# The gates' chain as steps inside the projection, and the adaLN products moved from VectorE to ScalarE and GpSimd

## What is computed

```
mod = silu(c) @ w_ada + b_ada                      # six sections of 1024 columns
z = h @ w_in + b_in                                # h: the normed tokens, 1024 + 256 context
q, k, v, o, gt, ga, gb = split(z)
gates = gt + b_gate                                # log i and forget pre-activations, two directions
u = ga * sigmoid(gb)                               # input of a 31 tap depthwise convolution
y = conv(u) + conv_b
lf = log_sigmoid(forget);  b = cumsum(lf) in each chunk of 128;  E = log i - b
# running maxima of E, a recurrence over the 10 chunks for the stabiliser m, and then
# exp(...) of four combinations: these are what the chunks of the mLSTM need
```

## Time and profile before

| | |
|---|---|
| median of 3 runs | 3208.84 us (3199.12 to 3208.93) |
| the profiled execution's time | 3209.92 us |
| its span | 3207.3 us |
| PE busy | 2741.5 us, 85% |
| DVE, ACT, POOL busy | 1672.9, 1164.2, 841.9 us |

### The profile page before, as it was taken

The page is one execution under the profiler, slowest core; times in us unless marked ns, Lnnn a source line. Parts: engine busy times, 40 slices in busy tenths (PEclk is TensorE's granted clock), DMA queues, the critical chain, the costliest instruction groups (busy, mean ns, idle before and its releaser), DMA issues. The chain is left out here.

```text
span 3207.3 us, 38552 instructions
## 1 busy us (share of the span) xinstructions
PE 2741.5 (85%) x11990; PEld 1944.7 (61%) x11991; DVE 1672.9 (52%) x2474; ACT 1164.2 (36%) x1598; POOL 841.9 (26%) x1036
## 2 busy tenths in 40 slices
PE   4899969497869999999999965999968999874997
PEld 4455435375357777777777753446654666763776
DVE  3667856565356567576576533145462111445653
ACT  1100023332056566566665542026322111214653
POOL 0100023221734334334333321067120000104333
PEclk9999966697989999999999987999989999976999
DMA  6331100133268788888798745000201110416972
GB/s 224 106 105 56 56 0 1 52 126 145 76 221 276 230 275 273 272 301 284 245 328 275 237 112 202 26 1 2 42 14 50 49 40 20 152 76 240 312 227 51
DMA packets 159179, 463.43 MB, mean 144 GB/s; under 512 B 37964, under 2 KB 67264, under 8 KB 138328
## 3 DMA queue, kind: packets, MB, share of 16 engines
q1 hardware_dynamic: 115816, 358.12, 30.1%
q0 software_dynamic: 43264, 104.02, 13.6%
HBM read 414.31 MB, written 91.62 MB: 158 GB/s over the span
## 5 line engine op out<-in xcount | busy, mean ns | idle before, releaser
L1855 DVE TENSOR_TENSOR moe_low<-moe_raw,moe_high 128x2048 fp32r<-128x2048 f32 x160 | 359.6, 2289 | 81.2 <-ACT moe_high L1800 81.2
L1765 PE MATMUL psum<-moe_high,moe_xg_high 128*128 128x512 f32 x960 | 390.2, 406 | 7.3 <-DVE moe_xg_low L1860 3.0
L1767 PE MATMUL psum<-moe_high,moe_xg_low 128*128 128x512 f32 x960 | 378.3, 394 | 0.0
L1766 PE MATMUL psum<-moe_low,moe_xg_high 128*128 128x512 f32 x960 | 375.7, 391 | 0.0
L1800 ACT ACTIVATE moe_high<-moe_raw 128x2048 fp32r<-128x2048 f32 x160 | 297.6, 1915 | 0.1
L1701 POOL DMA_INDIRECT moe_acc<-moe_y_blk,moe_is_now x97 | 214.5, 2211 | 299.4 <-DMA moe_acc<-moe_y_blk,moe_is_now 267.6
L1812 ACT ACTIVATE moe_y_blk<-psum,row_w 128x1024 f32 x124 | 138.2, 1115 | 235.6 <-DMA moe_acc<-moe_y_blk,moe_is_now 125.9
L1739 PE MATMUL psum<-ident,moe_xg 128*128 128x128 f32 x976 | 135.8, 284 | 95.2 <-DMA moe_xg<-moe_rows,moe_ig_now 95.0
L1752 PE MATMUL psum<-moe_high_down,moe_hid_high 128*128 x488 | 207.3, 425 | 11.6 <-DVE moe_hid_low L1864 10.7
L1765 PEld LDWEIGHTS psum<-moe_high,moe_xg_high 128*128 128x128 f32 x960 | 181.6, 189 | 44.8 <-issue 5.9
L1767 PEld LDWEIGHTS psum<-moe_high,moe_xg_low 128*128 128x128 f32 x960 | 181.0, 189 | 43.2
(11 more groups left out here) (578 smaller groups left out, 5043.2 us busy)
## 6 DMA issues: line engine op xcount, KB each, us to landing
moe_raw<-in_we_gate SPq DMA_DIRECT2D x64, 1024.0 KB, 7.8
moe_raw<-in_we_up SPq DMA_DIRECT2D x64, 1024.0 KB, 11.0
moe_raw<-in_we_down SPq DMA_DIRECT2D x64, 1024.0 KB, 7.6
moe_raw<-in_w_e_gate SPq DMA_DIRECT2D x16, 1024.0 KB, 6.9
moe_raw<-in_w_e_up SPq DMA_DIRECT2D x16, 1024.0 KB, 9.9
moe_raw<-in_w_e_down SPq DMA_DIRECT2D x16, 1024.0 KB, 8.2
w_ring<-in_w_in SPq DMA_DIRECT2D x12, 1024.0 KB, 7.6
wada<-in_w_ada SPq DMA_DIRECT2D x8, 1024.0 KB, 10.7
```

What stands on the lines that cost most here:

```text
L1765: pe.matmul(to, x_hi, R(of_k(w_hi, k)), start=(k == 0), stop=False)
L1766: pe.matmul(to, x_hi, R(of_k(w_lo, k)), start=False, stop=False)
L1767: last = pe.matmul(to, x_lo, R(of_k(w_hi, k)), start=False, stop=(k == KD - 1))
L1855: dve.tensor_tensor(R(low[:, at:at + 2048]), raw[r][:, part], hi, ALU.subtract).then_inc(w_low, 1)
```

## The change

`multiply` moves to ScalarE: it scales each of a half's four pieces into one of two `products` buffers, and signals. A new `add` on GpSimd copies or adds each product into `part`. GpSimd does the `add` of half q-2 in `load`, ahead of the DMA of half q. The two slots and the products now lie in `s.x` (tiles 2 to 6) and not in a buffer of their own; as `sig_o` uses tiles 4 to 7 of `s.x`, DVE waits for the last add before the first o entry. The gain row gets two buffers.

The plan changes: ADA4 stands behind v0 and gt0, ADA5 and ADA6 in channel group 2, ADA7 behind v5 and gt5, and group 3 has no ada entry. Between group 3's four tiles and behind them stand four new entries, `gate` 0 to 3. They hold what `stage_gates` did, cut at PE's steps (class `Gates`; the arithmetic is the same, its buffers lie in `hcT`): the gather and the logarithms run behind the last gt. `stage_gates` and its block are gone.

```diff
--- before.py
+++ after.py
@@ class LaterSections @@
-    def __init__(self, s, at, slots, part, gain_row):
-        self.s, self.at, self.slots, self.part, self.gain_row = s, at, slots, part, gain_row
+    def __init__(self, s, at, slots, products, part, gain_row):
+        self.s, self.at, self.slots, self.products, self.part, self.gain_row = s, at, slots, products, part, gain_row
+        self.product_ready, self.added = sem(s, "ada_product_ready"), sem(s, "ada_added")
         self.ada_in = [sem(s, f"ada_in{i}") for i in range(2)]
-        self.rows_in, self.gain_in = sem(s, "ada_rows_in"), sem(s, "ada_gain_in")
+        self.rows_in, self.gain_in = sem(s, "ada_rows_in"), [sem(s, f"ada_gain_in{i}") for i in range(2)]
         self.ada_used, self.finished = sem(s, "ada_used"), sem(s, "ada_finished")
 
...
         for q in range(2 * self.TILES):
             j, kh = divmod(q, 2)
             if q >= 2:
-
+                self.add(pool, q - 2)
                 pool.wait_ge(self.ada_used, q - 1)
             c0 = 2 * D + j * 512
             pool.dma_start(self.slots[q % 2], src[kh][:, :, c0:c0 + 512]).then_inc(self.ada_in[q % 2], 16)
             if kh == 0 and (2 + j // 2) % 3 == 2:
-                if n_gain:
-
-                    pool.wait_ge(self.finished, n_gain if n_gain < 3 else self.TILES - 1)
+                if n_gain >= 2:
+                    pool.wait_ge(self.finished, n_gain - 1)
                 name = ("g_post_mix", "g_post_ffn")[n_gain // 2]
-                pool.dma_start(self.gain_row[:, :], A[name][0:1, (j % 2) * 512:(j % 2) * 512 + 512].to_broadcast([P, 512])).then_inc(self.gain_in, 16)
+                pool.dma_start(self.gain_row[:, j % 2, :], A[name][0:1, (j % 2) * 512:(j % 2) * 512 + 512].to_broadcast([P, 512])).then_inc(self.gain_in[j % 2], 16)
                 n_gain += 1
 
-    def multiply(self, dve, q):
-
-        s, c = self.s, self.s.dve_c
+        for q in range(2 * self.TILES - 2, 2 * self.TILES):
+            self.add(pool, q)
+
+    def multiply(self, act, q):
+
+        s = self.s
+        kh = q % 2
+        act.wait_ge(self.ada_in[q % 2], 16 * (q // 2 + 1))
+        for k in range(self.KH):
+            n = self.KH * q + k
+            if n >= 2:
+                act.wait_ge(self.added, n - 1)
+            act.activation(self.products[:, n % 2, :], self.slots[q % 2][:, k, :], ACT.Copy,
+                           scale=s.cond[:, kh * self.KH + k, 0:1]).then_inc(self.product_ready, 1)
+        act.wait_ge(self.product_ready, self.KH * (q + 1))
+        act.sem_inc(self.ada_used, 1)
+
+    def add(self, pool, q):
+
         j, kh = divmod(q, 2)
-        dve.wait_ge(self.ada_in[q % 2], 16 * (q // 2 + 1))
+        to = self.part[:, j % 2, :]
         if kh == 0 and j >= 2:
-
-            dve.wait_ge(self.tile_done, self.at[j - 2] + 1)
-        to = self.part[:, j % 2, :]
+            pool.wait_ge(self.tile_done, self.at[j - 2] + 1)
         for k in range(self.KH):
-            w, scale = self.slots[q % 2][:, k, :], s.cond[:, kh * self.KH + k, 0:1]
+            n = self.KH * q + k
+            pool.wait_ge(self.product_ready, n + 1)
             if kh == 0 and k == 0:
-                c.link(dve, dve.tensor_scalar(to, w, scale, None, ALU.mult))
+                pool.tensor_copy(to, self.products[:, n % 2, :]).then_inc(self.added, 1)
             else:
-                c.link(dve, dve.scalar_tensor_tensor(to, w, scale, to, ALU.mult, ALU.add))
-        dve.sem_inc(self.ada_used, 1)
+                pool.wait_ge(self.added, n)
+                pool.tensor_tensor(to, to, self.products[:, n % 2, :], ALU.add).then_inc(self.added, 1)
 
     def tensor(self, pe, j, bank):
         s = self.s
-        pe.wait_ge(self.ada_used, 2 * (j + 1))
+        pe.wait_ge(self.added, 2 * self.KH * (j + 1))
         if (2 + j // 2) % 3 == 2:
             return pe.matmul(bank[:, :], s.ones[:, :], self.part[:, j % 2, :], start=True, stop=True)
         for m in range(4):
@@ -314,10 +329,10 @@
         if section % 3 == 2:
             h = section // 3
             dve.wait_ge(self.rows_in, 32)
-            dve.wait_ge(self.gain_in, 16 * (2 * h + half + 1))
+            dve.wait_ge(self.gain_in[half], 16 * (h + 1))
             to = s.gpost[:, h, half * 512:(half + 1) * 512]
             c.link(dve, dve.tensor_tensor(to, bank[:, :], to, ALU.add))
-            c.link(dve, dve.tensor_tensor(to, to, self.gain_row[:, :], ALU.mult))
+            c.link(dve, dve.tensor_tensor(to, to, self.gain_row[:, half, :], ALU.mult))
...
@@ def project_plan @@
     gab = lambda m: [("gb", m, 0), ("ga", m, 0), None, ("gb", m, 1), ("ga", m, 1), None]
+    last = [entry for i, part in enumerate((("gb", 3, 0), ("ga", 3, 0), ("gb", 3, 1), ("ga", 3, 1))) for entry in (part, ("gate", i, 0))]
     v = lambda t0, t1: [(kind, t, 0) for t in range(t0, t1) for kind in ("v", "gt")]
     plan = gab(0) + [("qk", m, n) for n in range(3) for m in range(4) if n < 2 or m >= 2]
-    plan += gab(1) + v(0, STEPS // 2) + gab(2) + v(STEPS // 2, STEPS) + gab(3)
+    plan += gab(1) + v(0, 1) + [None] + v(1, STEPS // 2) + gab(2) + v(STEPS // 2, STEPS // 2 + 1) + [None] + v(STEPS // 2 + 1, STEPS) + last
     plan += [("o", t, 0) for t in range(NT)] + [("kt", t, 0) for t in range(STEPS)]
...
@@ def stage_project @@
-                nc.sbuf_tensor("ada_slot", [P, KD // 2, 512], F32) as slot, nc.sbuf_tensor("ada_part", [P, 2, 512], F32) as part, \
-                nc.sbuf_tensor("ada_gain", [P, 512], F32) as gain_row:
+                nc.sbuf_tensor("ada_part", [P, 2, 512], F32) as part, \
+                nc.sbuf_tensor("ada_gain", [P, 2, 512], F32) as gain_row:
             at = [i for i, entry in enumerate(plan) if entry[0] == "ada"]
-            spare = s.x[:, 2:4, :].rearrange("p t (a n) -> p (t a) n", n=512)
-            later = LaterSections(s, at, (spare, slot[:, :, :]), part, gain_row)
+            slots = [s.x[:, t:t + 2, :].rearrange("p t (a n) -> p (t a) n", n=512) for t in (2, 4)]
+            later = LaterSections(s, at, slots, s.x[:, 6, :].rearrange("p (a n) -> p a n", n=512), part, gain_row)
...
+                    elif kind == "gate":
+                        last = gates.tensor(pe, a, bank)
...
                 for i, (kind, a, n) in enumerate(plan):
-                    if i in parts_at:
-                        later.multiply(dve, parts_at[i])
-                    taps({"kt": 1, "gt": 1, "ada": 0}.get(kind, 4))
+                    taps({"kt": 1, "gt": 1, "ada": 0, "gate": 0}.get(kind, 4))
                     if kind in by_act:
                         continue
...
+                        dve.sem_inc(moved_v, 1)
+                        continue
+                    if kind == "gate":
+                        gates.vector(dve, a, bank)
+                        c.wait(dve)
                         dve.sem_inc(moved_v, 1)
                         continue
...
+                        if i == first["o"]:
+                            dve.wait_ge(later.added, 2 * later.KH * later.TILES)
...
+                    if i == last_of["gt"]:
+                        dve.wait_ge(moved_v, place[i])
+                        gates.logs(dve)
                 taps(TAPS)
+                dve.wait_ge(gates.exps_ready, 4)
...
+                    if i in parts_at:
+                        later.multiply(act, parts_at[i])
+                    if i == last_of["gt"]:
+                        gates.scalar_logs(act)
+                    if (kind, a) == ("gate", 3):
+                        gates.scalar_exps(act)
...
+                gates.reduce(pool)
...
-def stage_gates(s):
...
+class Gates:
+
+    def __init__(self, s):
+        self.s = s
+        room = s.hcT.rearrange("p k c -> p (k c)")
+        self.V = {n: room[:, i * NCOL:(i + 1) * NCOL].rearrange("p (j d h) -> p j d h", j=STEPS, d=2) for i, n in enumerate(self.NAMES)}
+        self.ET = room[0:NCOL, 1024:1024 + 3 * P].rearrange("p (c n) -> p c n", c=3)
+        self.abs_ready, self.logs_ready, self.lf_ready = (sem(s, f"g_{x}") for x in ("abs_ready", "logs_ready", "lf_ready"))
+        self.e_ready, self.e_max, self.scans_ready, self.mt_ready, self.exps_ready = (
+            sem(s, f"g_{x}") for x in ("e_ready", "e_max", "scans_ready", "mt_ready", "exps_ready"))
+
...
+    def tensor(self, pe, step, bank):
+        s, flat, ET = self.s, self.flat, self.ET
+        if step == 0:
+            pe.wait_ge(self.lf_ready, 1)
+            for i, w in enumerate((s.tri_le, s.tri_ge, s.ones)):
+                last = pe.matmul(bank[:, i * P:i * P + NCOL], w[:, :], flat(self.V["FG"]), start=True, stop=True)
+        elif step == 1:
+            pe.wait_ge(self.e_ready, 1)
+            last = pe.transpose(bank[0:NCOL, 0:P], flat(s.E), s.ident[:, :])
+        elif step == 2:
+            pe.wait_ge(self.scans_ready, 2)
+            for d in range(2):
+                last = pe.transpose(bank[:, d * P:d * P + NCOL], ET[:, 1 + d, :], s.ident[0:NCOL, 0:NCOL])
+        else:
+            pe.wait_ge(self.mt_ready, 1)
```

(15 more changed lines are left out.)

137 lines of the change are left out of this document (52 added, 85 removed).

## The result

Median of 8 runs 3217.66 us (3211.66 to 3225.87), the kernel before beside it 3204.67 us (3197.12 to 3208.93): ratio 1.0044, 95% interval 1.0031 to 1.0057. The change makes the kernel slower, by about 13 us. The profiled execution took 3223.96 us, its span is 3222.2. What lies around the span is 1.8 us here and 2.6 before, so it is not the same for every kernel: the span grew by 14.9 us and the profiled time by 14.0.

What follows compares the result with a forecast made beforehand. PE, always busy in the projection, was taken as the bound. 5.8 + 1.8 + 9.8 + 9.8 + 1.7 - 16.4 = +12.5 us, giving 3221.3 us on the median's scale, range 3206 to 3232.

Steps and rivals of the forecast that it cites:

- ADA0: First ada entry of the projection: sums finish later, PE starts at 118.2 and not at 112.46, +5.8 us.
- ADA4 and ADA7: Behind v0, gt0 and v5, gt5: each stalls PE 7.1 us plus 2.7 of low clock, 9.8 us each.
- The stage leaves, at nothing but PE's steps: Between projection and mLSTM: the 16.4 us stage goes, its chain covered by group 3's tiles; PE's steps cost +1.7.
- The rival in which the chain isn't hidden: At the gate entries: PE waits, the 16.4 us shrink by 1 to 6; 0.18 together with a longer low clock.
- POOL's 7.69 us stay: At the mLSTM's start: POOL's first scaling of v still comes 7.69 us after POOL is free.
- The odd halves: ADA1, 2, 3, 5, 6: odd half behind ACT's sigmoid, 0.2 to 0.4 us stall each, 1.8 together.
- a tap and an add take whole turns: In v0 and v5: DVE taps and POOL adds alternate whole operations, 1.3 us each, stalling PE 7.1 us.
- The clock: Behind the pauses before ADA4 and ADA7: granted clock falls near 0.5, costing 2.7 us each.
- The rival in which the clock stays low for a whole further tile: Pauses of 7 to 11 us cost a further half-rate tile, three times: about +20; 0.18 together with an unhidden chain.
- The stages behind: Stages behind the projection keep their length; a change of it would show the prediction wrong.
- main case: Whole kernel: taps and adds take turns, the terms sum to +12.5 us; 3216 to 3228, chance 0.55.
- rival without turns: No turns between taps and adds: ADA4 5.4 + 2.7, ADA7 3.2 + 1.4, +5.6 us in all, 3214.4; chance 0.17.

Runs made afterwards that it cites:

- gates_lead: gates_only with ADA4 and ADA7 two token tiles later and their halves issued four and two entries ahead; 0.9945 against the kernel before.
- engines_only: Products and sums on ScalarE and GpSimd, slots in x, with the plan and gates' stage of the kernel before; 1.0025 against that kernel.
- no_taps: The changed kernel with the taps of v0, gt0, v5 and gt5 left for later entries; one time, 3220.48 us.
- load_later: The changed kernel with SP's loads of group 2's weights waiting for gt1; one time, 3215.8 us.
- late_ada: The changed kernel with ADA4 and ADA7 two token tiles later; 0.9982 against the kernel before.
- best3: best with ADA4 and ADA7 two token tiles later and their halves issued four and two entries ahead; 0.9926 against the kernel before.
- after_again: The changed kernel, unchanged, run again on another chip; 3217.04 us against 3208.11 for the kernel before, 1.0035.
- gates_only: The changed kernel with the products back on DVE and no add, keeping its plan and gate entries; 0.9986 against the kernel before.
- best: gates_only with ADA0 behind all four tiles of group 0 and ADA1 two tiles further; 0.9966 against the kernel before.

## Why the prediction was right

The predicted 3221.3 us stand against 3217.66, inside the range and slower as forecast. The rise was 13.0 us (14.0 between the profiled executions) where 12.5 were predicted; the 3.6 us between the two times come from the median before, 3204.67 with eight runs and 3208.84 with the three that the prediction had. Its main mechanisms were seen: the hidden chain, the later start of ADA0, and pauses before ADA4 and ADA7 with a slow clock behind them. Its picture of how taps and adds share their time was not, and its sizes erred in opposite ways.

- *The stage leaves, at nothing but PE's steps:* right. -16.3 and +1.1 for -16.4 and +1.7. The tightest cover, the gather and the logarithms, had 1.7 us to spare: DVE wrote the last input at 368.86 + 0.24 = 369.10, and PE came to the first gate entry at 370.75. The rival in which the chain isn't hidden did not come about.
- *POOL's 7.69 us stay:* right, 7.38 in after and 7.26 in gates_lead. Over all the profiles the gap is 6.7 to 7.7 us. The Trainium skill (GPSIMD Engine Reference, Instruction dispatch) has about 6 us, with no instruction in the profile, for the first call of newly loaded GpSimd code; these rows are longer. The trace agrees in kind: two rows MODIFY_POOL_CONFIG of POOL's sequencer stand at the start of the gap, the first scaling 7.3 us behind them. The maximum has two such rows of its own, 49 us before it runs, where they cost nothing:

```profile
L832 POOLq MODIFY_POOL_CONFIG  x2: 11/11/11, 453.2 to 453.2; - x2
...
L691 POOLq MODIFY_POOL_CONFIG  x2: 6/6/6, 326.1 to 326.1; - x2
```

But two more stand at 107.9, before the first add, and that started at 108.06; the rows alone do not make a gap. The maximum itself took 1.51 us and not 0.59, at a place where it costs nothing. No run tried to take this gap away; PE's wait of 11.66 us behind it is the largest left between the projection and the mLSTM.

- *ADA0:* +6.0 to its start, predicted 5.8; engines_only shows it alone. The slow tiles behind it cost 0.9 us less than before.
- *The odd halves:* the recorded waits are 0.39 to 0.49, at and above the top of the 0.2 to 0.4; but from tile to tile each costs 0.5 to 0.8 us. In the kernel before, an entry starts some 0.15 us before the one ahead of it ends (ADA3 at 220.86, the tile until 207.05 + 13.98 = 221.03), and across an idle time this overlap is gone. 3.4 for 1.8.
- *ADA4 and ADA7:* the terms that were mis-sized, 8.3 and 7.4 for 9.8 each; the pauses themselves were 5.7 and 5.3 us where 7.1 were taken. The step behind it, that a tap and an add take whole turns, is not what was measured. In the kernel after, 8.66 us of POOL hold four adds and 4.38 us of DVE hold two taps: 2.2 us for a pair, not 2.6. Alone an add takes 1.26 us, 1.38 with the wait for its semaphore, and a tap 1.28. They slow each other a good deal (no_taps: 3.1 us less pause at ADA7), and still overlap by some 0.4 us a pair., from which the turns were read, are one such pair with another operation on DVE, and by its own sum that pair too ended 0.26 us early (691.18 for 691.44). By the Trainium skill (SBUF - State Buffer, SBUF: two separate sides) a DVE operation with two inputs in SBUF or a GpSimd operation that reads SBUF, whichever starts first, holds the shared port pair for the whole instruction, and the other blocks; my estimate for a pair by that rule is 1.28 + 1.26 = 2.5 us. The rows measure 2.2, and the measurement decides.
- In place of the turns, the transfer of q9 held ADA4: POOL had finished q8 and waited 1.75 us for it. The landing was predicted at 230 for an issue at 221.2, 8.8 us; 8.3 were measured from the issue to ACT's first product. This was in the sum, but not as the term that ends last. With the transfer out of the way (load_later) the sums hold ADA4 only 0.5 us less long. At ADA7 the stretched sums alone held PE: POOL waited only 0.17 us before its last four adds.
- *The clock:* right in kind, too large. The granted clock was 0.64 and 0.75 around ADA4's end, and not near 0.5, and v1 and v6 took 1.5 and 1.1 us more; with the ada entry itself (1.84 for 1.02, 2.04 for 1.10) that is 2.4 and 2.0, where 2.7 was taken from the longer fall behind ADA0. The rival in which the clock stays low for a whole further tile did not come: the tile behind each pause lost 1.5 and 1.1 us, the gt behind it nothing, and the window inside v6 is at 0.96.
- *The stages behind:* the prediction let them keep their length, and named a change of it as a sign that it is wrong. In the profile they took 5.5 us more, so by that sign it failed there, and this makes up for the 3.6 us that the projection came out below the sum. Were the projection all, the result would have been near +9 us, just under the 9.6 that the prediction took as the least that can be told from no change. Whether the change has a part in it stays open. For it: the stretch of the experts took 1082.4 and 1080.7 us in the two profiles of the kernel after against 1077.4 and 1073.3 before. Against it: kernels with the same lines there and the same plan of buffers took 1075.8 (load_later), 1077.4 (engines_only) and 1078.0 (late_ada), best3, the fastest of all, took 1081.1, and in after_again the median rose by 8.9 us where the mark alone rose by 10.0. With single profiles that differ by 4 us in one kernel it can't be settled.

That the total was near is thus partly luck: in the projection alone the measured +8.9 lies midway between the main case (+12.5) and the rival without turns (+5.6), as a pair of 2.2 us lies between turns and no turns. The prediction laid ADA4 and ADA7 on ACT, POOL and the taps; gates_only says that with the products left on DVE the same plan pauses 3.6 and 4.9 us there. The marks put a size on it: gates_only gives back 13.6 of the 15.2 us that the gates' move is worth, against the 15.7 that ADA4 and ADA7 cost in the kernel after. The price of these two belongs to the place in the plan first and to the engines second, and the prediction did not cost the two apart.

## What to carry to other kernels

When an entry is moved in a list that several in-order engines run, look up what its operands' producers stand behind in their own queues at the new place, and how long the entry just before it covers; here a gt of 1.7 us took the place of a ga of 6.9. To move work off an engine that is not the bound bought nothing here (engines_only, 1.0025), and it pays the slower engine's time wherever the consumer already waits. A pause of the bounding engine is cheap to find and dear to keep: those of 3.6 to 5.7 us before ADA4 and ADA7 cost 1.7 to 3.9 us more in the slow steps behind them (3.3 and 1.7 in gates_only, 2.4 and 2.0 in the kernel after, 3.9 behind best's pause of 3.58), and the edits that took two of them away (gates_only to gates_lead, 0.9986 to 0.9945) gave 13 us, nearly as much as hiding the whole chain.

## What the runs showed of the hardware

- A DVE tap of 128x1024 and a POOL add of 128x512, both float32 in SBUF, take 1.28 and 1.26 us alone (1.38 from add to add, with the semaphore) and about 2.2 us each side by side: less than the 2.5 of strict turns, more than either alone.
- POOL copies 128x512 in 0.62 us; ACT scales it from SBUF with a column of scales in 0.72.
- A 1 MB transfer issued by POOL reached its consumer 5.5 us after the issue with no load of SP's beside it (load_later), and 8.3 us with SP's four of 512 KB (after).
- POOL's first 128x129 scaling of the mLSTM starts 6.7 to 7.7 us after POOL is free in every kernel, whether the partition maximum ended 8.5 us or 75.5 us before that stage. Its sequencer's two MODIFY_POOL_CONFIG rows stand at the start of the gap, 1 us into the stage, and not in the idle time before it. That the maximum makes them necessary is not shown: no kernel ran without it.
